# Order of weight splits against block sums and gates in the feed-forwards of a two-layer encoder

## Chip, cores and metric
One core of a Trainium2 chip runs the whole program in one launch. The metric is the device time in microseconds of that core. The engines are PE (TensorE, matmuls), DVE (VectorE), ACT (ScalarE), POOL (GpSimd) and SP (SyncE, which here only issues DMAs). Each runs its own queue of instructions in order; they meet through semaphores.

## What is computed
The trunk has two layers over 256 tokens of width 1024, in float32. Each layer is a feed-forward, a mixer (neighbourhood attention and pooling) and a second feed-forward:

```
def swiglu(h, w_gate, w_up, w_down):
    return (jax.nn.silu(h @ w_gate) * (h @ w_up)) @ w_down

for l in range(DEPTH):                                    # DEPTH = 2
    x = x + 0.5 * swiglu(rms_norm(x, ffn1_norm[l]), w_gate1, w_up1, w_down1)
    ...                                                   # mixer
    x = x + 0.5 * swiglu(rms_norm(x, ffn2_norm[l]), w_gate2, w_up2, w_down2)
```

The inner width is 2816. So the program has four feed-forwards, FF1 and FF2 of each layer.

## The kernel before
**Split numbers.** Every float32 operand is split into a high part (rounded to the matmul's float32r form) and a low part (the rest), and a product is the three matmuls high x high, high x low and low x high (`split_products`, L1397, L1398 and L1400). For a unit of weights (128 x 2048 words, 1 MB) SP loads `w_raw`, ACT writes `w_hi` in two halves (`split_hi`, L627, or with the norm's gains L634), and DVE writes `w_lo = w_raw - w_hi` in two halves (`split_lo`, L984, or L995). The semaphores `raw_ready`, `hi_ready` and `lo_ready` of each slot order these. SP reloads a slot's `w_raw` when the low part of the unit in it is done (`wait_raw_free`).

**Chunks.** A feed-forward is cut into 11 chunks of 256 inner columns. An ordinary chunk takes two gate-and-up units, in slots a and b, one for each half of the 1024 inputs; for each of the two token tiles t PE computes 8 k-tiles (`ordinary`), then ACT takes the silu (`silu_of`, L712), DVE multiplies (`gate`, L1045), PE transposes (L1506), ACT and DVE store the high and low parts (`store_gt_hi` L701, `store_gt_lo` L1051), and PE multiplies with the down unit in slot d (`whole_down`).

**Pairs.** Chunks 0 and 1 go first. Then a loop runs two bodies (`ff_body`, `BODIES = 2`) of four chunks: an ordinary one, a pair whose gate and up products are formed with seven block products instead of eight (`seventh`), and another ordinary one. Chunk 2 is the ordinary one at the start of the first body. The pair needs sums of weight blocks and of activation blocks. Slots e and f serve the pair: e's unit is split, then DVE adds f's raw unit onto e's raw unit (`add_units(e, f)`, L1131), and that sum is split into slot f (`sum_hi`, L643). POOL adds another unit onto f by an accumulating DMA once `sum_ready` says that the first sum is done (L506).

**Activation blocks.** In `ff_stage`, ACT and DVE bring the normed activations to scaled form (`scale_x` L721, `add_low_x` L1085), split them (`x_hi` L731, `x_lo` L1071), sum their blocks in place by four dependent additions on DVE (`sum_blocks`, L1098 to L1107), and split the sums (`s_hi` on ACT, L739, `s_lo` on DVE, L1115). The unsummed blocks serve chunk 2 (PE waits for `x_lo_ready` 4n + 2 ahead of the loop); the summed ones are first read in the pair's products (PE waits for 4n + 4 there).

**Order.** Nothing plans at run time. What runs when on each engine is the order in which the code issues it, written out by hand for ACT, DVE, PE, SP and POOL, with waits at each step. The change touches ACT's and DVE's `ff_body` and `ff_stage`.

Of the kernel before, what the change touches and what calls it, by code (L numbers as in the profile page):

```python
# [103 lines left out]
def trunk(nc, x, ffn1_norm, ffn1_w_gate, ffn1_w_up, ffn1_w_down, mix_norm, w_in, rpb, w_pool,  # L104
# [8 lines left out]
    with ctx:  # L113
# [186 lines left out]
        def raw_no(layer, stage, slot, k):  # L300

            return layer * RAWS_PER_LAYER[slot] + (RAWS_BEFORE[stage][slot] + k)
# [13 lines left out]
        def ord_no(layer, ff, i):  # L316

            return ff_no(layer, ff) * N_ORDINARY + i
# [261 lines left out]
        def _(act):  # L580
# [56 lines left out]
            def sum_hi(slot, raw, ready, used):  # L637

                act.wait_ge(*ready)
                act.wait_ge(*used)  # L640
                for h in range(2):
                    part = slice(h * HALF, (h + 1) * HALF)
                    nc.scalar.activation(w_hi[slot][:, part], w_raw[raw][:, part], ACT.Copy  # L643
                                         ).then_inc(hi_ready[slot], 2)
# [65 lines left out]
            def silu_of(layer, ff, i, t):  # L710
                act.wait_ge(gu_ready[t], ord_no(layer, ff, i) + 1)
                nc.scalar.activation(silu[:, t, :], ps[:, t, 0:FC], ACT.Silu, scale=rstd[:, t, :]  # L712
                                     ).then_inc(silu_ready[t], 1)
# [21 lines left out]
            def s_hi(layer, ff):  # L735

                act.wait_ge(s_summed, 4 * (ff_no(layer, ff) + 1))
                for t in range(TT):
                    nc.scalar.activation(  # L739
                        xs_hi[:, 2 * t + 4:2 * t + 6, :, :].rearrange("p o k q -> p (o k q)"),  # L740
                        normed[:, t, :], ACT.Copy).then_inc(x_hi_ready, 1)
# [11 lines left out]
            def ff_body(layer, ff, j):  # L753
                a, b = ff["g"]
                d, e, f = ff["d"], SLOT_E, SLOT_F
                i = 4 * j + 2
                n = pair_no(layer, ff, j)

                def plain(slot, raw, m, used=None):
                    split_hi(slot, raw, raw_no(layer, ff["stage"], raw, m), used)  # L760

                plain(d, d, 3 * j + 1, (down_used, down_no(layer, ff, i)))
                plain(e, e, 2 * j, (g0_used, ord_no(layer, ff, 2 * j + 1) + 1))
                store_gt_hi(layer, ff, i - 1)
                silu_of(layer, ff, 2 * j + 2, 0)
                sum_hi(f, e, (sum_ready, 3 * n + 1), (gu_ready[1], ord_no(layer, ff, 2 * j + 1) + 1))
                plain(a, a, 2 * j + 3, (g0_used, ord_no(layer, ff, 2 * j + 2) + 1))
                silu_of(layer, ff, 2 * j + 2, 1)
                plain(b, b, 3 * j + 3)
                plain(d, d, 3 * j + 2, (down_used, down_no(layer, ff, i + 1)))  # L770
                copy_m(BANK_X, 7 * n + 1, p1)
                copy_m(BANK_Z, 7 * n + 2, m5)
                sum_hi(e, e, (sum_ready, 3 * n + 2), (m_ready, 7 * n + 1))
                store_gt_hi(layer, ff, i)
                sum_hi(f, f, (t3_loaded, 32 * n + 32), (m_ready, 7 * n + 2))
                act.wait_ge(combined, 7 * n + 1)
                silu_pair(c11, 0, 0)
                sum_hi(a, a, (sum_ready, 3 * n + 3), (m_ready, 7 * n + 3))
                plain(e, b, 3 * j + 4, (m_ready, 7 * n + 5))
                act.wait_ge(combined, 7 * n + 4)  # L780
                silu_pair(p1, 0, 1)
                plain(f, f, 2 * j + 1, (m_ready, 7 * n + 6))
                act.wait_ge(combined, 7 * n + 6)
                silu_pair(m5, 1, 0)
                plain(b, d, 3 * j + 3, (m_ready, 7 * n + 4))
                act.wait_ge(combined, 7 * n + 7)
                silu_pair(u, 1, 1)
                plain(d, e, 2 * j + 1, (down_used, down_no(layer, ff, i + 2)))
                store_gt_hi(layer, ff, i + 1, 1)
                silu_of(layer, ff, 2 * j + 3, 0)  # L790
                store_gt_hi(layer, ff, i + 2)
                plain(a, a, 2 * j + 4, (m_ready, 7 * n + 7))
                silu_of(layer, ff, 2 * j + 3, 1)
                plain(b, b, 3 * j + 5, (down_used, down_no(layer, ff, i + 3)))

            def ff_stage(layer, ff, following=None):
                a, b = ff["g"]
                d = ff["d"]
                stage = ff["stage"]
                scale_x(layer, ff, range(4))  # L800
                for t in range(TT):
                    act.wait_ge(scaled_ready[t], layer * STAGES + (stage + 1))
                silu_of(layer, ff, 0, 0)
                split_hi(a, a, raw_no(layer, stage, a, 1), (g0_used, ord_no(layer, ff, 0) + 1),
                         (stage, layer, 0))
                silu_of(layer, ff, 0, 1)
                split_hi(b, b, raw_no(layer, stage, b, 1), gains_of=(stage, layer, 4))
                scale_x(layer, ff, range(4, KT))
                split_hi(d, d, raw_no(layer, stage, d, 0), (down_used, down_no(layer, ff, 1)))
                x_hi(layer, ff)  # L810
                store_gt_hi(layer, ff, 0)
                silu_of(layer, ff, 1, 0)
                s_hi(layer, ff)
                split_hi(a, a, raw_no(layer, stage, a, 2), (g0_used, ord_no(layer, ff, 1) + 1))
                silu_of(layer, ff, 1, 1)
                split_hi(b, b, raw_no(layer, stage, b, 2))
                with act.Fori(0, BODIES) as j:
                    ff_body(layer, ff, j)
                if ff is FF1:
                    load_params(layer)  # L820
                    load_tables(layer)
                elif layer == DEPTH - 1:
                    load_final_gain()
                split_hi(d, d, raw_no(layer, stage, d, 3 * BODIES + 1),
                         (down_used, down_no(layer, ff, LAST)))
                store_gt_hi(layer, ff, LAST - 1)
                silu_of(layer, ff, 2 * BODIES + 2, 0)
                split_hi(a, a, raw_no(layer, stage, a, 2 * BODIES + 3),
                         (g0_used, ord_no(layer, ff, 2 * BODIES + 2) + 1))
                silu_of(layer, ff, 2 * BODIES + 2, 1)  # L830
                store_last_gt_hi(layer, ff, 0)
                if following:
                    following()
                store_last_gt_hi(layer, ff, 1)
# [136 lines left out]
        def _(dve):  # L971
# [149 lines left out]
            def ff_body(layer, ff, j):  # L1121
# [19 lines left out]
                                                   ALU.mult, ALU.mult).then_inc(pair_gated, 1)  # L1141

                lo(d, 3 * j + 1, d)
                lo(e, 3 * j, e)
                store_gt_lo(layer, ff, i - 1)
                gate(layer, ff, 2 * j + 2, 0)

                dve.wait_ge(raw_ready[f], raw_count(f, raw_no(layer, ff["stage"], f, 2 * j)))
                dve.wait_ge(lo_ready[e], 4 * unit_no(layer, ff["stage"], e, 3 * j) + 5)
# [49 lines left out]
            def ff_stage(layer, ff, following=None):  # L1199
                a, b = ff["g"]  # L1200
                add_low_x(layer, ff, range(4))
                for t in range(TT):
                    dve.wait_ge(scaled_ready[t], layer * STAGES + (ff["stage"] + 1))
                gate(layer, ff, 0, 0)
                unit(layer, ff, a, 1, gains_from=0)
                gate(layer, ff, 0, 1)
                unit(layer, ff, b, 1, gains_from=4)
                add_low_x(layer, ff, range(4, KT))
                unit(layer, ff, ff["d"], 0)
                x_lo(layer, ff)  # L1210
                store_gt_lo(layer, ff, 0)
                sum_blocks(layer, ff)
                gate(layer, ff, 1, 0)
                unit(layer, ff, a, 2)
                gate(layer, ff, 1, 1)
                unit(layer, ff, b, 2)
                s_lo(layer, ff)
                with dve.Fori(0, BODIES) as j:
                    ff_body(layer, ff, j)
                unit(layer, ff, ff["d"], 3 * BODIES + 1)  # L1220
                store_gt_lo(layer, ff, LAST - 1)
                gate(layer, ff, 2 * BODIES + 2, 0)
                unit(layer, ff, a, 3 * BODIES + 3)
                gate(layer, ff, 2 * BODIES + 2, 1)
                store_last_gt_lo(layer, ff, 0)
                if following:
                    following()
                store_last_gt_lo(layer, ff, 1)
# [665 lines left out]
```

## Time and profile before

| | us |
|---|---|
| median of 3 runs (lowest, highest) | 921.59 (921.36, 921.64) |
| profiled execution, its own time | 921.39 |
| its span | 919.6 |
| PE busy (share of span) | 906.5 (99%) |
| PE weight loads busy | 741.1 (81%) |
| DVE busy | 703.5 (77%) |
| ACT busy | 540.1 (59%) |
| HBM read over the span | 179.11 MB, 197 GB/s |

The span is the profiled part between first and last instruction; the execution's own time is 1.8 us longer. Busy time of PE counts matmuls that overlap in its pipeline, so each shows about 0.39 us although they start closer together. The engines wait for each other throughout; idle time matters where it is PE's.

### The profile page before, as it was taken

Reading aid. Unit: us, or ns where it says so; the run is one execution under the profiler, and the core shown is the slowest. Engines: PE = TensorE matmul, PEld = TensorE weight load, DVE = VectorE, ACT = ScalarE, POOL = GpSimd, SP = SyncE. Lnnn points to the kernel's source line nnn. Section 1 sums busy time; section 2 is a strip of 40 time slices with the busy share of each in tenths; the row PEclk is TensorE's granted clock in tenths of the full one; section 3 lists DMA queues with packets and bytes.
Section 4 is the critical chain, followed back from the end, with each engine's and each line's share of the span. In section 5 each row is a group of like instructions: output and inputs, shape, how many; then the busy total and the mean of one; then the engine's idle time right before and its main releaser. Section 6 shows DMA issues by size and latency. Waiting matters only on the chain.

```text
span 919.6 us, 12693 instructions
## 1 busy us (share of the span) xinstructions
PE 906.5 (99%) x4217; PEld 741.1 (81%) x4217; DVE 703.5 (77%) x946; ACT 540.1 (59%) x793; POOL 47.0 (5%) x78
## 2 busy tenths in 40 slices
PE   8999999999999999999999999999999999999997
PEld 6788888887778788888887888888877887888886
DVE  5899688459757898697488987965787588968944
ACT  7765466457638566555385655544675476656633
POOL 1010010010001010100010101010100001001000
PEclk9999999999999999999999999999999999999999
DMA  7876757755245857775268577676434277676631
GB/s 251 302 193 242 274 110 260 240 174 183 92 136 168 290 110 277 237 222 183 91 227 277 127 277 227 207 212 235 138 143 143 82 271 215 217 261 161 246 114 46
DMA packets 131101, 180.76 MB, mean 197 GB/s; under 512 B 7664, under 2 KB 107296, under 8 KB 131056
## 3 DMA queue, kind: packets, MB, share of 16 engines
q1 hardware_dynamic: 117744, 165.43, 52.2%
q0 software_dynamic: 9984, 11.22, 7.4%
q10 hardware_dynamic: 3328, 3.54, 1.2%
q8 instruction: 25, 0.41, 0.2%
q14 instruction: 20, 0.16, 0.1%
HBM read 179.11 MB, written 2.07 MB: 197 GB/s over the span
## 4 chain that ended last, share of the span: by engine, by line
PE 89%; DVE 5%; ACT 3%; DMA 1%; issue 1%; SPq 1%; POOLq 0%; ACTq 0%; POOL 0%; DVEq 0%
PE ps L1397 27%; PE ps L1400 26%; PE ps L1398 26%; PE ps L1506 2%; DVE w_lo L984 1%; PE ps L1458 1%; PE ps L1407 1%; PE ps L1408 1%; DVE xs_lo L1071 1%; PE ps L1480 1%; PE ps L1696 1%; ACT w_hi L634 1%; ACT w_hi L627 1%; PE ps L1712 1%; PE ps L1724 1%
## 5 line engine op out<-in xcount | busy, mean ns | idle before, releaser
L984 DVE TENSOR_TENSOR w_lo<-w_raw,w_hi 128x1024 fp32r<-128x1024 f32 x184 | 216.6, 1218 | 97.2 <-ACT w_hi L627 96.7
L627 ACT ACTIVATE w_hi<-w_raw 128x1024 fp32r<-128x1024 f32 x168 | 167.2, 1049 | 94.3 <-PE ps L1400 94.3
L1397 PE MATMUL ps<-w_hi,gt_hi 128*128 128x512 f32 (+1 forms) x356 | 138.9, 390 | 0.0
L1398 PE MATMUL ps<-w_lo,gt_hi 128*128 128x512 f32 (+1 forms) x356 | 137.7, 387 | 0.0
L1397 PE MATMUL ps<-w_hi,xs_hi 128*128 128x512 f32 x288 | 114.5, 398 | 4.9 <-DVE w_lo L984 4.9
L1400 PE MATMUL ps<-w_hi,xs_lo 128*128 128x512 f32 x288 | 112.4, 390 | 0.0
L1398 PE MATMUL ps<-w_lo,xs_hi 128*128 128x512 f32 x288 | 112.3, 390 | 0.0
L1397 PE MATMUL ps<-w_hi,xt_hi 128*128 128x512 f32 x272 | 110.0, 404 | 0.2 <-DVE xt_lo L1009 0.2
L1400 PE MATMUL ps<-w_hi,gt_lo 128*128 128x512 f32 (+1 forms) x356 | 109.9, 387 | 0.0
L1398 PE MATMUL ps<-w_lo,xt_hi 128*128 128x512 f32 x272 | 106.1, 390 | 0.0
L1400 PE MATMUL ps<-w_hi,xt_lo 128*128 128x512 f32 x272 | 101.1, 391 | 0.0
L995 DVE SCALAR_TENSOR_TENSOR w_lo<-w_raw,gains,w_hi 128x512 fp32r<-128x512 f32 x128 | 88.0, 745 | 15.7 <-ACT w_hi L634 13.3
L634 ACT ACTIVATE w_hi<-w_raw,gains 128x512 fp32r<-128x512 f32 x120 | 76.6, 714 | 4.9 <-PE ps L1400 4.8
L1400 PEld LDWEIGHTS ps<-w_hi,gt_lo 128*128 128x128 f32 x356 | 66.8, 188 | 13.7
L1397 PEld LDWEIGHTS ps<-w_hi,gt_hi 128*128 128x128 f32 x356 | 66.9, 188 | 13.6 <-DVE gt_lo L1051 0.4
L1398 PEld LDWEIGHTS ps<-w_lo,gt_hi 128*128 128x128 f32 x356 | 66.9, 188 | 13.2
L1397 PEld LDWEIGHTS ps<-w_hi,xs_hi 128*128 128x128 f32 x288 | 54.1, 188 | 17.2 <-DVE w_lo L984 6.6
L1400 PEld LDWEIGHTS ps<-w_hi,xs_lo 128*128 128x128 f32 x288 | 54.1, 188 | 11.6
L1398 PEld LDWEIGHTS ps<-w_lo,xs_hi 128*128 128x128 f32 x288 | 54.2, 188 | 10.6
L1397 PEld LDWEIGHTS ps<-w_hi,xt_hi 128*128 128x128 f32 x272 | 51.1, 188 | 14.1 <-issue 3.0
L1400 PEld LDWEIGHTS ps<-w_hi,xt_lo 128*128 128x128 f32 x272 | 51.0, 188 | 11.0
L1398 PEld LDWEIGHTS ps<-w_lo,xt_hi 128*128 128x128 f32 x272 | 51.2, 188 | 8.9
(151 smaller groups left out, 1488.7 us busy)
## 6 DMA issues: line engine op xcount, KB each, us to landing
w_raw<-in_ffn_w_down_dram SPq DMA_DIRECT2D x72, 512.0 KB, 5.4
w_raw<-in_ffn_w_gate_dram SPq DMA_DIRECT2D x62, 512.0 KB, 4.2
w_raw<-in_ffn_w_up_dram SPq DMA_DIRECT2D x62, 512.0 KB, 5.3
w_raw<-in_w_in_dram SPq DMA_DIRECT2D x32, 512.0 KB, 4.7
w_raw_f<-in_ffn_w_gate_dram SPq DMA_DIRECT2D x16, 512.0 KB, 5.3
w_raw_f<-in_ffn_w_up_dram SPq DMA_DIRECT2D x16, 512.0 KB, 6.2
w_raw_e<-in_ffn_w_down_dram SPq DMA_DIRECT2D x16, 512.0 KB, 7.0
w_raw<-in_w_out_dram SPq DMA_DIRECT2D x16, 512.0 KB, 5.1
```

The costliest lines, as they stand in the source:

```text
L627: nc.scalar.activation(w_hi[slot][:, part], w_raw[raw][:, part], ACT.Copy).then_inc(hi_ready[slot], 2)
L634: nc.scalar.activation(w_hi[slot][:, part], w_raw[raw][:, part], ACT.Copy, scale=g).then_inc(hi_ready[slot], 1)
L984: nc.vector.tensor_tensor(w_lo[slot][:, part], w_raw[raw][:, part], w_hi[slot][:, part].bitcast(F32), ALU.subtract).then_inc(lo_ready[slot ...
L995: nc.vector.scalar_tensor_tensor(w_lo[slot][:, part], w_raw[slot][:, part], g, w_hi[slot][:, part].bitcast(F32), ALU.mult, ALU.subtract).t ...
L1071: nc.vector.tensor_tensor(xs_lo[:, 2 * t:2 * t + 2, :, :].rearrange("p o k q -> p (o k q)"), normed[:, t, :], xs_hi[:, 2 * t:2 * t + 2, :, ...
L1397: nc.tensor.matmul(o, hi, wh, start=start, stop=False)
L1398: nc.tensor.matmul(o, hi, wl, start=False, stop=False)
L1400: last = nc.tensor.matmul(o, lo, wh, start=False, stop=bool(stop))
L1407: nc.tensor.matmul(out, hi, w_hi_part, start=start, stop=False)
L1408: nc.tensor.matmul(out, hi, w_lo_part, start=False, stop=False)
L1458: last = nc.tensor.matmul(ps[:, bank, :], xt_lo[:, 0, 4 * a + k, :], w_hi[slot][:, k * BANK:(k + 1) * BANK], start=False, stop=(a, k) == ( ...
L1506: last = nc.tensor.transpose(ps[:, 6, (k * TT + t) * P:(k * TT + t + 1) * P], source[:, t, k * P:(k + 1) * P], ident[:, :])
```

## The change
It moves calls in two functions, on ACT and on DVE alike, and adds and removes none.

In the loop's body, the split of e's first unit goes behind the store of the transposed chunk and the silu (ACT) or gate (DVE) of the body's ordinary chunk, first token tile. Ahead of the loop, both splits of chunk 2's units (`a` and `b`, unit 2), with the silu and gate of chunk 1's two tiles between them, go ahead of `s_hi` on ACT and ahead of `sum_blocks` on DVE.

```diff
@@ ACT, ff_body
                 plain(d, d, 3 * j + 1, (down_used, down_no(layer, ff, i)))
-                plain(e, e, 2 * j, (g0_used, ord_no(layer, ff, 2 * j + 1) + 1))
                 store_gt_hi(layer, ff, i - 1)
                 silu_of(layer, ff, 2 * j + 2, 0)
+                plain(e, e, 2 * j, (g0_used, ord_no(layer, ff, 2 * j + 1) + 1))
                 sum_hi(f, e, (sum_ready, 3 * n + 1), (gu_ready[1], ord_no(layer, ff, 2 * j + 1) + 1))
@@ ACT, ff_stage
                 silu_of(layer, ff, 1, 0)
-                s_hi(layer, ff)
                 split_hi(a, a, raw_no(layer, stage, a, 2), (g0_used, ord_no(layer, ff, 1) + 1))
                 silu_of(layer, ff, 1, 1)
                 split_hi(b, b, raw_no(layer, stage, b, 2))
+                s_hi(layer, ff)
                 with act.Fori(0, BODIES) as j:
@@ DVE, ff_body
                 lo(d, 3 * j + 1, d)
-                lo(e, 3 * j, e)
                 store_gt_lo(layer, ff, i - 1)
                 gate(layer, ff, 2 * j + 2, 0)
+                lo(e, 3 * j, e)
@@ DVE, ff_stage
                 store_gt_lo(layer, ff, 0)
-                sum_blocks(layer, ff)
                 gate(layer, ff, 1, 0)
                 unit(layer, ff, a, 2)
                 gate(layer, ff, 1, 1)
                 unit(layer, ff, b, 2)
+                sum_blocks(layer, ff)
                 s_lo(layer, ff)
```

## Rows read from the trace of the kernel before

**Rows 1.** The page, part 1: busy time, share of the span, instructions.
```profile
PE 906.5 (99%) x4217; PEld 741.1 (81%) x4217; DVE 703.5 (77%) x946; ACT 540.1 (59%) x793; POOL 47.0 (5%) x78
```

**Rows 2.** Waits of PE: total us, times, longest us.
```profile
PE ps L1397 <- DVE w_lo L984: 4.9, 4, 1.4
```

**Rows 3.** Timeline of PE, layer 0, FF1 and FF2: start, length, idle before.
```profile
40.15 0.50 PE L1397 MATMUL ps<-w_hi,xs_hi 128*128 128x512 f32 x1 [1.35 <-DVE w_lo L984]
...
296.91 0.48 PE L1397 MATMUL ps<-w_hi,xt_hi 128*128 128x512 f32 x1
...
306.11 0.62 PE L1400 MATMUL ps<-w_hi,gt_lo 128*128 128x512 f32 x2
...
307.47 0.61 PE L1400 MATMUL ps<-w_hi,gt_lo 128*128 128x512 f32 x2
309.27 0.50 PE L1397 MATMUL ps<-w_hi,xs_hi 128*128 128x512 f32 x1 [1.18 <-DVE w_lo L984]
309.60 0.40 PE L1398 MATMUL ps<-w_lo,xs_hi 128*128 128x512 f32 x1
309.84 0.39 PE L1400 MATMUL ps<-w_hi,xs_lo 128*128 128x512 f32 x1
```

**Rows 4.** Timeline of DVE, layer 0, FF2, ahead of the loop.
```profile
302.03 0.68 DVE L1098 TENSOR_TENSOR normed<-normed 128x512 f32<-128x512 f32 x1
...
307.99 2.36 DVE L984 TENSOR_TENSOR w_lo<-w_raw,w_hi 128x1024 fp32r<-128x1024 f32 x2 [2.70 <-ACT w_hi L627]
310.26 0.48 DVE L1045 SCALAR_TENSOR_TENSOR gated<-ps,rstd_scaled,silu 128x256 f32<-128x256 f32 x1
...
312.93 2.35 DVE L1115 TENSOR_TENSOR xs_lo<-normed,xs_hi 128x1024 fp32r<-128x1024 f32 x2
315.20 2.35 DVE L984 TENSOR_TENSOR w_lo<-w_raw,w_hi 128x1024 fp32r<-128x1024 f32 x2
```

**Rows 5.** Timeline of ACT, layer 0, FF2, ahead of the loop.
```profile
300.00 0.46 ACT L712 ACTIVATE silu<-ps,rstd 128x256 f32<-128x256 f32 x1
304.93 2.01 ACT L739 ACTIVATE xs_hi<-normed 128x1024 fp32r<-128x1024 f32 x2 [4.46 <-DVE normed L1107]
306.84 1.99 ACT L627 ACTIVATE w_hi<-w_raw 128x1024 fp32r<-128x1024 f32 x2
```

**Rows 6.** Timeline of SP's queue: the request for chunk 2's first unit.
```profile
292.60 0.51 SPq L357 DMA_DIRECT2D w_raw<-in_ffn_w_up_dram  x1
```

**Rows 7.** The page, part 6: DMA issues, KB each, us to landing.
```profile
w_raw<-in_ffn_w_up_dram SPq DMA_DIRECT2D x62, 512.0 KB, 5.3
```

**Rows 8.** Busy time in two stretches, layer 0, FF2: first body, second body.
```profile
core 0: us, PE busy (x) PEld busy (x) DVE busy (x) ACT busy (x) POOL busy (x), PEclk, DMA share, GB/s
315.20:353.90 38.70, 38.70 (x175) 31.83 (x173) 37.20 (x38) 22.25 (x28) 2.67 (x2) 1.00 0.71 211
377.90:415.90 38.00, 38.00 (x173) 31.46 (x172) 34.77 (x35) 22.28 (x29) 4.26 (x4) 1.00 0.68 198
```

**Rows 9.** Timeline of DVE and PE, first body, the last unit in f.
```profile
352.74 2.35 DVE L984 TENSOR_TENSOR w_lo_f<-w_raw_f,w_hi_f 128x1024 fp32r<-128x1024 f32 x2
...
353.67 0.39 PE L1400 MATMUL ps<-w_hi_e,xs_lo 128*128 128x512 f32 x1
354.00 0.50 PE L1397 MATMUL ps<-w_hi_f,xs_hi 128*128 128x512 f32 x1
```

**Rows 10.** Timeline of ACT, DVE and PE, second body of the same feed-forward.
```profile
380.74 0.47 ACT L712 ACTIVATE silu<-ps,rstd 128x256 f32<-128x256 f32 x1
...
381.87 2.28 DVE L1131 TENSOR_TENSOR w_raw_e<-w_raw_e,w_raw_f 128x2048 f32<-128x2048 f32 x1
...
398.25 2.36 DVE L984 TENSOR_TENSOR w_lo_e<-w_raw_e,w_hi_e 128x1024 fp32r<-128x1024 f32 x2 [1.08 <-ACT w_hi_e L643]
...
415.05 2.35 DVE L984 TENSOR_TENSOR w_lo_f<-w_raw_f,w_hi_f 128x1024 fp32r<-128x1024 f32 x2
...
418.65 0.39 PE L1397 MATMUL ps<-w_hi_f,xs_hi 128*128 128x512 f32 x1
```

**Rows 11.** POOL's accumulating DMAs (line 506), the line on their landing.
```profile
DMA to landing us min/median/max: 6.1/7.2/10.2
```

## The prediction, made before the changed kernel was run

> **What bounds the kernel now.** I read the page's first section, then what TensorE waited for, then the timelines around those waits. PE is busy 906.5 us of a span of 919.6 [rows 1]. Busy time alone proves little, so the spacing counts: two equal places of a down projection, six matmuls apart, start at 306.11 and 307.47 [rows 3], 1.36 us or 0.227 us a matmul, with nothing between them. So PE's queue is the bound, and only time in which it stands still can be won by a reordering. Its largest wait is for DVE's `w_lo` of an ordinary unit: 4 times, 4.9 us together [rows 2]. There are four feed-forwards, and each has this wait once, at the first matmul of the loop's first body. In the second feed-forward (layer 0, FF2) the last matmuls of the down projection start at 307.47, so the next could start at 307.47 + 2 x 0.227 = 307.92; it starts at 309.27, and the one behind it 0.33 instead of 0.23 later [rows 3]. Each such stall costs 1.35 + 0.10 = 1.45 us, in the first feed-forward 0.17 more, since its idle time is 1.35 and not 1.18 [rows 3]. All four: 4 x 1.45 + 0.17 = 6.0 us.
>
> Why does the low part of chunk 2's first unit come so late? DVE's queue up to 307.99 [rows 4]: four block sums from 302.03, a gate, and then 2.70 us idle until the split's high part is there. ACT's queue [rows 5]: silu at 300.00, done about 300.36; the high part of the summed blocks (`s_hi`) at 304.93, held by the sums; only then the unit's high part at 306.84, and DVE follows 1.15 us later. The unit waits for block sums it does not use.
>
> **Part 1: chunk 2 ahead of the sums** (twice in ff_stage). Nothing is added or dropped; I replay both queues with the spacings that the rows give.
> ACT: behind the silu, a's split starts at 300.36. Its raw data was requested at 292.60 [rows 6] and lands in about 5.3 us [rows 7], so 297.9. Its old contents are free once PE has done k-tile 3 of chunk 1's second half, about 299.9 by the row at 296.91 [rows 3] plus 12 x 0.23 plus one latency. Two halves take 1.91 (the distance 304.93 to 306.84 of two equal operations [rows 5]). The next silu needs PE's end of the chunk, about 302.7, and b's split runs from about 303.2 to 305.2.
> DVE: gate 302.03 to 302.43; a's low part (2.27, from 307.99 to 310.26 [rows 4]) to 304.70; gate (310.26 to 312.93 is a gate and an equal split, so 0.40) to 305.10; b's low part to 307.37. PE wants a at 307.92 and b 2.7 us later: 3.2 us to spare. The stall goes in full.
> Then the sums: 2.90 from their start to the start of s_hi (302.03 [rows 4], 304.93 [rows 5]), so s_hi starts at 310.27; `s_lo` starts 1.15 later at 311.42 and takes 2.27, to 313.69. The loop's first split, d, started on DVE at 315.20 [rows 4] and now starts at 313.69, if ACT has it: s_hi to 312.18, first half of d ready for DVE at 313.33. Behind s_hi on ACT stand d's split and the body's gt_hi and silu; PE wants d only after two products of 5.4 us. So DVE's whole chain moves up 1.51, because its idle 2.70 becomes 1.18. PE waits for the summed blocks only ahead of its first block product, three times 24 x 0.227 = 5.44 and some transposes after 307.92, so at about 324.7; s_lo has 11 us of cover, and without it would cost one for one.
> SP: the loads behind a's and b's low parts (`free(a, 3j+3)`, `free(b, 3j+3)`) go out about 5.7 us earlier, behind e, d and f in the same queue. Their own users come only after e's. What they could cost is bandwidth taken from d, e and f, which were requested first; at the one end that is 0, at the other it eats the 1.5 that DVE's chain gains. I take 0, because a load lands in about 5.3 us [rows 7] and those are out 4 us before. POOL's accumulating DMA waits for the e+f sum and moves with DVE's chain.
>
> **What is late next.** In the first body DVE is nearly the bound itself: 37.20 us busy out of 38.70 [rows 8]. At the pair's last unit f, DVE starts the low part at 352.74 and PE takes it at 354.00, when by the matmul at 353.67 it could have come at 353.90 [rows 9]. There PE is tied to DVE, so what survives this point is DVE's gain, 1.51, not PE's 1.45 (first feed-forward: 1.62). Hence 1.5 us for each feed-forward, 6.0 together. Bounds: DVE gaining only half (0.75 each) gives 3.0; DVE gaining 0.25 more removes this small stall of 0.1 + 0.1 too, 4 x 1.68 = 6.7.
>
> **Part 2: e's split behind gt and gate in every body.** First body: both orders have DVE full, so the e+f sum starts after the same work. ACT: d's high part to 314.1, `gt_hi` to 314.6, silu to 315.0, e's first half at 316.1; DVE: d to 315.96, gt_lo 316.56, gate 316.96, e to 319.23. The sum starts there as it would in the old order; price 0. Had the order stayed, gt_lo would come 2.27 later, but still ahead of PE's 319.3.
> Second body: here it costs DVE something, because e's split used to fill the time in which DVE waited for PE's transposes. Old: silu at 380.74, sum at 381.87 [rows 10]. New: silu done 381.10, e's low part from 382.25 to 384.52, sum at 384.52: 2.65 us later. Behind it stand everything DVE does up to the next wait, ACT's high part of f, POOL's accumulating DMA (landing in 10.2 us at most [rows 11]; ACT takes it 13 us behind), and SP's next load into b. At e's second low part DVE used to wait 1.08 for ACT at 398.25 [rows 10]; that absorbs as much, leaving about 1.5 late. The tightest user is f's last low part: 415.05 becomes 416.6, its first half done at 417.7; PE takes it at 418.65 [rows 10]. 0.9 us is left, and 1.5 at the unit before it. Price 0; uncovered it is one for one. If all 2.65 came through, 1.7 a feed-forward.
>
> **One rule weighed.** The second matmul after the stall follows at 0.33, the third at 0.24 [rows 3]; it does not run faster to catch up. A stall's end is therefore an end for everything behind.
> The Trainium skill, "TensorE: Matmul & The Clock Gate", section "Back-to-back issue gap", gives about 131 ns per matmul of 512 columns as what a real stream sustains. By that, PE would have 0.1 us a matmul in reserve, and the sum would be 0.
>
> **Sum.** Profiled execution 921.39 (span 919.6 and 1.8 around it). 921.39 - 6.0 = 915.4. It lies 0.2 below the median 921.59, so the new median is 915.4 to 915.6; I take **915.6**. Less than 0.2% (1.8 us) either way is what a measurement here cannot tell from no change.
>
> **Rivals.**
> 1. DVE or ACT gains less than PE, and the difference returns as a wait in the first body at f. For: the tie at 354.00. Against: the idle that disappears is plain. At 0.75 each: 918.4.
> 2. Second body, slower: e's split ahead of the sum delays the pair chain, PE waits at f's last low part. It decides from 0.9 us of lateness, and eats the whole gain from 0.9 + 1.5 = 2.4 us; the chain starts with 2.65. For: DVE is busy 34.77 of 38.00 there [rows 8]. Against: the 1.08 wait. If nothing is absorbed, 4 x 1.7 = 6.8 against 6.0: 922.2, slower; together with rival 1's loss 925.2.
> 3. Another condition holds the first body at 309.27 (raw data, an accumulation bank), so nothing is won: 921.4. Against: the row names DVE, and by the half of its 2.27 from 307.99 DVE's first half ended at 309.13, just before PE's start.
> 4. PE has reserve and had caught up anyway, so no change: 921.4. The spacing speaks against. (By the Trainium skill's 131 ns above, this one would hold; the trace does not agree.)
>
> **Chances.** Forecast 0.82; rival 1: 0.08; rival 2: 0.05; rival 3: 0.04; rival 4: 0.01. Faster by over 0.2%: forecast and rival 1, 0.90. Same: 0.07 (3, 4 and half of 2). Slower: 0.03 (the rest of 2). Range 914.7 to 918.2: below it the small stall of 6.7, above it most of rival 1.
>
> **What would show it.** The four waits of PE for `w_lo` of 1.2 to 1.35 us gone; DVE idle between sums and s_lo about 1.2 instead of 2.7; the same small wait for f in first bodies, about 0.2; e+f sums of the second bodies about 2.6 us after the gate, yet no PE wait there. Wrong if PE waits over 0.3 us in a second body, or if the loop still starts over 0.3 us after the first down projection.

## The result, and the profile after

The changed kernel takes 916.02 us in the median of 6 runs (915.74 to 916.33), the kernel before 921.50 beside it (921.35 to 921.72): a ratio of 0.9939, 95% interval 0.9929 to 0.9950, or 5.5 us less. The forecast was 915.6.

The waits of PE's matmuls in the changed kernel, in the form of [rows 2] (total us, times, longest us). The row with 4 times and 4.9 us is gone. The list shows no wait in the loop now; a wait of PE as short as the one at f has no row of its own and is read from the starts below:

```profile
PE ps L1833 <- DVE zeros L972: 1.5, 1, 1.5
PE ps L1397 <- DVE xt_lo L1009: 0.8, 1, 0.8
PE ps L1540 <- DVE xt_lo L1009: 0.6, 2, 0.4
```

These three are in the start and at norms, not in the changed code. In the chain that ended last PE's share is 94% here, after 89%. In the trace before, the chain runs through DVE and ACT ahead of each of the four loops. Here it does so ahead of none, and leaves PE only later in the first feed-forward, at f (84.02). The share itself proves little, though: a second profile of the same changed kernel (run a2 below) gives 88%. There the chain of the last feed-forward leaves PE at f and goes back through DVE and ACT to the block sums. The page's line of the changed kernel, that of a2, and two pieces of a2's chain:

```profile
PE 94%; DMA 2%; DVE 2%; ACT 1%; SPq 1%; issue 1%; POOLq 0%; DVEq 0%; POOL 0%; ACTq 0%
```
```profile
PE 88%; DVE 4%; ACT 3%; issue 2%; DMA 2%; SPq 1%; DVEq 0%; POOLq 0%; ACTq 0%; POOL 0%
...
755.43 0.61 DVE normed L1098
...
799.43 1.14 DVE w_lo_f L984
```

PE's timeline at the same place as [rows 3] (layer 0, FF2; start, length, no idle time):

```profile
306.67 0.62 PE L1400 MATMUL ps<-w_hi,gt_lo 128*128 128x512 f32 x2
307.12 0.39 PE L1397 MATMUL ps<-w_hi,xs_hi 128*128 128x512 f32 x1
307.35 0.39 PE L1398 MATMUL ps<-w_lo,xs_hi 128*128 128x512 f32 x1
```

The first matmul of the loop follows the down projection at 0.45 us, two spacings, and the next one at 0.23, so the slow restart is gone with the wait. DVE's timeline there, to be laid beside [rows 4]:

```profile
301.24 0.47 DVE L1045 SCALAR_TENSOR_TENSOR gated<-ps,rstd_scaled,silu 128x256 f32<-128x256 f32 x1
301.63 2.35 DVE L984 TENSOR_TENSOR w_lo<-w_raw,w_hi 128x1024 fp32r<-128x1024 f32 x2
...
306.56 0.68 DVE L1098 TENSOR_TENSOR normed<-normed 128x512 f32<-128x512 f32 x1
...
310.54 2.36 DVE L1115 TENSOR_TENSOR xs_lo<-normed,xs_hi 128x1024 fp32r<-128x1024 f32 x2 [1.13 <-ACT xs_hi L739]
312.82 2.35 DVE L984 TENSOR_TENSOR w_lo<-w_raw,w_hi 128x1024 fp32r<-128x1024 f32 x2
...
315.69 0.47 DVE L1045 SCALAR_TENSOR_TENSOR gated<-ps,rstd_scaled,silu 128x256 f32<-128x256 f32 x1
316.08 2.35 DVE L984 TENSOR_TENSOR w_lo_e<-w_raw_e,w_hi_e 128x1024 fp32r<-128x1024 f32 x2
318.47 2.29 DVE L1131 TENSOR_TENSOR w_raw_e<-w_raw_e,w_raw_f 128x2048 f32<-128x2048 f32 x1
```

The reader is to see two things. The unit's low part starts before the sums, 5.5 us ahead of PE, and DVE's idle time is 1.13 where it was 2.70. And the sum at 318.47 starts 2.39 us behind the start of e's low part, while anything else that follows such a split starts 2.27 behind it: 0.12 us more.

To compare stretches whatever happened before them, I take the time from the first matmul of the first down projection to the start of the second body in this feed-forward. It was 302.48 to 374.16 before, 71.68 us, and is 301.68 to 371.89 now, 70.21: 1.47 us less. Measured alike, the other three gain 1.41, 1.46 and 1.40, together 5.7. What follows in a feed-forward, from the second body on, takes the same in both kernels (75.99 us before, 75.98 now, up to the first down projection behind the second body).

### The profile page after: what moved, and what is told of

Read it like the earlier page. It is cut to its first block, busy times and chain, and to the rows that moved or that the text cites. A ratio compares the mean times of both kernels' runs of the same rounds, so it can differ in the third digit from the quotient of the medians.

```text
span 914.5 us, 12693 instructions
## 1 busy us (share of the span) xinstructions
PE 905.3 (99%) x4217; PEld 741.0 (81%) x4217; DVE 704.0 (77%) x946; ACT 539.3 (59%) x793; POOL 47.1 (5%) x78
## 4 chain that ended last, share of the span: by engine, by line
PE 94%; DMA 2%; DVE 2%; ACT 1%; SPq 1%; issue 1%; POOLq 0%; DVEq 0%; POOL 0%; ACTq 0%
PE ps L1397 28%; PE ps L1400 28%; PE ps L1398 28%; PE ps L1506 2%; DMA w_raw<-in_ffn_w_up_dram 1%; PE ps L1458 1%; PE ps L1407 1%; PE ps L1408 1%; PE ps L1480 1%; PE ps L1696 1%; PE ps L1712 1%; PE ps L1724 1%; PE ps L1740 1%; DMA w_raw_f<-in_ffn_w_up_dram 1%; SPq L376 0%
```

## The experiments

Each kernel is the kernel before or the changed kernel with the edit shown. Runs e1 to e4 ran together (the kernel before at 921.74 beside them), so did the changed kernel again, e1 again, e5 and e7 (921.87), and e6 and e8 (921.65). Code is cut: `...` stands for arguments, and a comment gives the real call where it matters.

**e1: part 1 alone.**
```diff
@@ changed kernel, ff_body, on ACT and DVE: back to the old order
+                plain(e, e, 2 * j, ...)      # lo(e, 3 * j, e) on DVE
                 store_gt_hi(layer, ff, i - 1)
                 silu_of(layer, ff, 2 * j + 2, 0)
-                plain(e, e, 2 * j, ...)
```


> Part 1 alone: chunk 2's splits ahead of the sums on ACT and DVE, e's split left where it was in the loop's bodies. Theory A (part 1 gives everything; part 2 costs a little, because the e+f sum then stands right behind e's low part and waits 0.12 us for its end, on a chain that in the first body is tied to PE): all four start waits gone, the wait at f in the first bodies 0.12 shorter, 4 x 0.12 = 0.5 us faster than the changed kernel, so 915.5; the e+f sums of the second bodies back to where they were. Theory B (part 2 is what keeps DVE's early move from being lost, for instance through the store of the low gated part): a wait of PE for gt_lo shows up in the first body, 916.5 to 918.

Measured: 915.58 (ratio 0.9933, 0.9919 to 0.9946). No wait for gt_lo appears in a body. The stretch above takes 301.14 to 371.22, 70.08 us. DVE's rows at the sum of the first body:

```profile
316.82 0.68 DVE L1051 TENSOR_TENSOR gt_lo<-ps,gt_hi 128x512 fp32r<-128x512 f32 x1
317.42 0.47 DVE L1045 SCALAR_TENSOR_TENSOR gated<-ps,rstd_scaled,silu 128x256 f32<-128x256 f32 x1
317.81 2.28 DVE L1131 TENSOR_TENSOR w_raw_e<-w_raw_e,w_raw_f 128x2048 f32<-128x2048 f32 x1
```

Here e's low part, which starts at 314.55 and takes 2.35, has been over for 0.9 us when the sum comes up, and the 0.12 is gone. So all of the gain is part 1's.

**e2: part 2 alone.** The counterpart: ff_body as changed, ff_stage as before.


> Part 2 alone: e's split behind store and gate in each body, the order ahead of the loop as before. Theory A: the four start waits stay (4.9 us), the first bodies' tie at f costs 0.12 more each, so 921.5 + 0.5 = 922.0, no wait of PE in the second bodies. Theory B: some gain of its own, 920 to 921. The rival of the prediction (second bodies run late): over 923.

Measured: 922.11 (ratio 1.0005, 0.9996 to 1.0014), 0.4 above the kernel before beside it. The four waits stay, and the stretch takes 302.82 to 374.61, 71.79, 0.11 more than before:

```profile
PE ps L1397 <- DVE w_lo L984: 4.9, 4, 1.3
```

The interval holds 1, so by the times alone it is no difference; the stretch in the trace has the expected sign and size. Second bodies show no wait: the rival of late second bodies did not come.

**e1 and the changed kernel side by side.**


> The changed kernel once more, to stand beside part 1 alone on the same chip and to show whether the 0.58 us by which its first profile was late before the first loop (33.64 against 33.06 us at the first down projection) belongs to it. Theory: it is the start's own scatter, and this profile shows some other value from 33.0 to 33.7; median 5.5 to 6.0 us under the kernel before. Rival: 33.6 again, as something in the changed program makes the start late.

> Part 1 alone once more, beside the changed kernel. Theory A: 0.4 to 0.6 us under it (the 0.12 us at the e+f sum of each first body). Rival: the same within 0.1, and the earlier difference was scatter between sessions.

Measured: the changed kernel 915.96 (915.93 to 916.25; ratio 0.9937), part 1 alone 915.46 (915.25 to 915.68; 0.9931). The two ranges of five runs do not touch: part 2 costs 0.5 us. By the stretches of the first profiles it is 0.10 to 0.13 in each of the four feed-forwards. The start of the first down projection, the last point ahead of any changed code that matters, in the kernel before, the changed one and the changed one again:

```profile
33.06 0.50 PE L1397 MATMUL ps<-w_hi,gt_hi 128*128 128x512 f32 x1
```
```profile
33.64 0.50 PE L1397 MATMUL ps<-w_hi,gt_hi 128*128 128x512 f32 x1
```
```profile
33.10 0.50 PE L1397 MATMUL ps<-w_hi,gt_hi 128*128 128x512 f32 x1
```

In all twelve profiles of this study it lies between 32.98 and 33.68, by no pattern that follows an edit. So 0.6 us of a single execution is the start's scatter, not the change.

**e3: ACT's half of part 1 alone.**
```diff
@@ kernel before, ACT, ff_stage; nothing else
                 silu_of(layer, ff, 1, 0)
-                s_hi(layer, ff)
                 split_hi(a, a, raw_no(layer, stage, a, 2), (g0_used, ord_no(layer, ff, 1) + 1))
                 silu_of(layer, ff, 1, 1)
                 split_hi(b, b, raw_no(layer, stage, b, 2))
+                s_hi(layer, ff)
```


> Only ACT's half of part 1: s_hi behind chunk 2's splits on ACT; DVE keeps the block sums ahead of them, and the bodies stay as before. If what made chunk 2 late was ACT's wait for the sums (theory A), DVE needs no reorder: it goes from the sums to the gate and the low part of a without the 2.7 us idle, is ready 1.4 us ahead of PE, and finds s_hi ready at s_lo. DVE's chain then gains 2.7 instead of 1.5 us, which also lifts the tie at f in the first bodies (0.15 wait and 0.1 restart each): 4 x (1.45 + 0.22) = 6.7 us off 921.5, 914.8, no small wait for f left. Theory C (the DVE reorder is what gives the gain, as 2.9 us of sums stand ahead of the low part): a start wait of up to 1 us each stays, 917 to 919.

Measured: **914.55** (914.43 to 914.85; ratio 0.9920, 0.9907 to 0.9934), the lowest median of all. DVE, with its order as before, has no idle time from the sums to the loop:

```profile
300.63 0.68 DVE L1098 TENSOR_TENSOR normed<-normed 128x512 f32<-128x512 f32 x1
...
303.80 2.35 DVE L984 TENSOR_TENSOR w_lo<-w_raw,w_hi 128x1024 fp32r<-128x1024 f32 x2
306.07 0.47 DVE L1045 SCALAR_TENSOR_TENSOR gated<-ps,rstd_scaled,silu 128x256 f32<-128x256 f32 x1
306.46 2.34 DVE L984 TENSOR_TENSOR w_lo<-w_raw,w_hi 128x1024 fp32r<-128x1024 f32 x2
308.73 2.35 DVE L1115 TENSOR_TENSOR xs_lo<-normed,xs_hi 128x1024 fp32r<-128x1024 f32 x2
311.00 2.35 DVE L984 TENSOR_TENSOR w_lo<-w_raw,w_hi 128x1024 fp32r<-128x1024 f32 x2
```

The low part starts at 303.80 and PE needs it at 306.52, with its first half (1.22 long) done 1.5 us before. `s_hi`, which ACT starts at 303.56, was finished long ago when DVE comes to `s_lo`. The tie at f is gone as well; PE takes f with the ordinary length of 0.39, 1.3 us after its first low half is done:

```profile
348.54 2.35 DVE L984 TENSOR_TENSOR w_lo_f<-w_raw_f,w_hi_f 128x1024 fp32r<-128x1024 f32 x2
...
351.01 0.39 PE L1397 MATMUL ps<-w_hi_f,xs_hi 128*128 128x512 f32 x1
```

The stretch takes 301.08 to 371.02, 69.94, 1.74 less than before. The other half, the sums behind the splits on DVE with `s_hi` still ahead of them on ACT, was not tried: by the code, each engine would wait for the other and never go on.

**e4: ACT's half with part 2.**


> ACT's half of part 1 together with part 2. Theory A: with DVE 1.2 us further ahead, the tie at f is lifted, so the 0.12 us that part 2 costs on DVE is hidden: the same as ACT's half alone, 914.8. If part 2 costs anything in the second bodies, this is slower than ACT's half alone by that much.

Measured: 914.69 (914.52 to 914.99; 0.9922), 0.14 above e3 and with ranges that overlap; the stretch 69.93. Where DVE is ahead, part 2's cost is hidden.

**e5: 0.57 us more on DVE in the changed kernel.**
```diff
@@ DVE, ff_body
                 gate(layer, ff, 2 * j + 2, 0)
+                nc.vector.tensor_tensor(pad[:, :], zeros[:, 0:PAGE_PAD].bitcast(F32),
+                                        zeros[:, 0:PAGE_PAD].bitcast(F32), ALU.add)
                 lo(e, 3 * j, e)
```


> The changed kernel with one useless DVE addition (128 x 480, about 0.57 us of DVE's time) ahead of e's low part in each body. Theory A (tie at f in first bodies, 0.87 us of slack in second ones): 0.57 comes through in each of four first bodies and nowhere else: 4 x 0.57 = 2.3 us slower than the changed kernel, 918.3. Rival (no tie, DVE has room in both): no change, 916. Rival (second bodies tied too): 4.6 us slower.

Measured: 918.28 (917.96 to 918.70), 2.3 over the changed kernel beside it. The stretch of the first body grows by 0.60 (301.64 to 372.45, 70.81), in the four feed-forwards together by 2.3, and nothing is lost in second bodies. So the size is what the theory said, but not the place. PE is already 0.39 late at 330.06, behind the transposes of the ordinary chunk; in the first feed-forward the trace puts the same wait down to ACT's copy of a block product (L746). I had not named that meeting point. Only the rest is lost at f:

```profile
330.06 0.49 PE L1399 MATMUL ps<-w_hi,xs_hi 128*128 128x512 f32 x1
...
352.31 0.50 PE L1399 MATMUL ps<-w_hi_f,xs_hi 128*128 128x512 f32 x1 [0.17 <-DVE w_lo_f L984]
```

**e6, e7, e8: the same addition once, twice and three times a body, in the kernel without the tie (e4).**
```diff
@@ DVE, ff_body; e6 the first, e7 the first two, e8 all three
+                nc.vector.tensor_tensor(pad[:, :], ...)     # ahead of lo(e, 3 * j, e)
+                nc.vector.tensor_tensor(pad[:, :], ...)     # ahead of add_units(e, b)
+                nc.vector.tensor_tensor(pad[:, :], ...)     # ahead of add_units(a, e)
```


> ACT's half of part 1 with part 2, with one useless DVE addition (0.57 us) ahead of e's low part in each body. Theory A (0.86 us of slack at f in all bodies): hidden, 914.7 as without it. Rival (chain tied to PE elsewhere): 2.3 us or 4.6 us slower.

> ACT's half of part 1 with part 2 (no tie in first bodies), with two such useless additions in each body: one ahead of e's low part, one ahead of the e+b sum, 1.14 us together. Its profile without them shows 0.86 us between the end of f's first low half and PE's use of it, in first and second bodies alike. Theory A: 1.14 - 0.86 = 0.28 us and about 0.1 for the restart come through in all eight bodies: 8 x 0.38 = 3.0 us over the 914.7 without them, 917.7. Rival (the second bodies absorb it by other waits): 1.5 us over, 916.2. Rival (slack is larger than read): no change.

> The same kernel with three such additions in each body, the third ahead of the a+e sum, 1.71 us together. Theory A: 1.71 - 0.86 = 0.85 and 0.1 for the restart in all eight bodies, 7.6 us over 914.7: 922.3, which is slower than the kernel before. This prices the prediction's second rival: how late the pair's chain must be to eat the gain. Rival (second bodies absorb): 3.8 over, 918.5.

Measured: 914.90 (914.69 to 914.96), 916.45 (916.40 to 916.57) and 920.77 (920.38 to 921.70), so 0.2, 1.8 and 6.1 us over e4's 914.69. (e4 is of another group; the kernel before stood at 921.65 to 921.87 in all of them.) One is hidden; two and three come out lower than expected. The size was misread, not the place. PE's rows at f in e7, then in e8, first and second body:

```profile
351.18 0.39 PE L1404 MATMUL ps<-w_hi_e,xs_lo 128*128 128x512 f32 x1
351.48 0.50 PE L1401 MATMUL ps<-w_hi_f,xs_hi 128*128 128x512 f32 x1
...
415.88 0.39 PE L1404 MATMUL ps<-w_hi_e,xs_lo 128*128 128x512 f32 x1
416.15 0.50 PE L1401 MATMUL ps<-w_hi_f,xs_hi 128*128 128x512 f32 x1
```
```profile
352.13 0.39 PE L1406 MATMUL ps<-w_hi_e,xs_lo 128*128 128x512 f32 x1
352.92 0.50 PE L1403 MATMUL ps<-w_hi_f,xs_hi 128*128 128x512 f32 x1 [0.40 <-DVE w_lo_f L984]
...
418.15 0.50 PE L1403 MATMUL ps<-w_hi_f,xs_hi 128*128 128x512 f32 x1 [0.39 <-DVE w_lo_f L984]
```

In e7 f starts 0.30 and 0.27 behind the matmul ahead of it instead of 0.23, and with the slow restart each body loses about 0.2; eight bodies make 1.6, against 1.8 measured. Two sizes were misread. The first stands in e4's own DVE row:

```profile
314.73 2.36 DVE L984 TENSOR_TENSOR w_lo_e<-w_raw_e,w_hi_e 128x1024 fp32r<-128x1024 f32 x2 [0.27 <-ACT w_hi_e L627]
```

With e's split behind the silu on ACT, DVE has to wait for its high part, and the first addition fell partly into that. In e4 e's low part starts 0.74 behind the start of the gate ahead of it, in e7 0.96, so the addition's 0.57 moved it by 0.22 only, and both additions move f's low part by 0.79. The second is the slack. Wherever PE is held at f in these traces, it starts 1.26 to 1.28 behind the start of f's low part. In e4 it starts 1.99 behind, so the slack is 0.72 and not the 0.86 of the expectation:

```profile
349.13 2.35 DVE L984 TENSOR_TENSOR w_lo_f<-w_raw_f,w_hi_f 128x1024 fp32r<-128x1024 f32 x2
...
351.12 0.39 PE L1397 MATMUL ps<-w_hi_f,xs_hi 128*128 128x512 f32 x1
```

So 0.79 - 0.72 = 0.07 is left, and e7's first body shows it: 0.30 - 0.23. The third addition adds nearly its full 0.57. In e8 f starts 0.79 behind the matmul ahead of it, 0.56 late, and the restart costs 0.1 more; by the stretches first bodies lose 0.75 to 0.97 and second ones 0.72 to 0.77, together 6.2. First and second bodies lose nearly alike, so the rival in which second bodies absorb more falls.

## Why the prediction was right, step by step

**The start waits.** All four gone, each with its restart. That the unit waited for sums it does not use was the cause, and e3 sharpens it: what held the unit was ACT's wait in front of it, not the 2.9 us of sums on DVE. PE gained 1.45 at this point in layer 0's FF2 and 1.66 in the first feed-forward (forecast 1.62).

**DVE's chain moves up 1.51.** Against the start of the down projection (302.48 before, 301.68 now) the loop's first split moved from 315.20 to 312.82, by 2.38 - 0.80 = 1.58. The idle 1.18 came out as 1.13.

**The tie at f.** Right, and it set the size. f's low part moved from 352.74 to 350.48, 2.26 - 0.80 = 1.46, and PE's use of it from 354.00 to 351.75, 2.25 - 0.80 = 1.45. DVE lost 0.12 on the way, between 312.82 and 350.48. That is the term that the prediction had at 0. In this feed-forward PE's gain at the start and DVE's at f are the same to 0.01, so it can't tell which of them counts. The first one can: its 1.66 shrink to 1.45 at f, DVE's gain there, and PE's wait at f grows. In the trace before and in the changed kernel's, f starts 0.31 and 0.52 behind the matmul ahead of it:

```profile
84.58 0.39 PE L1400 MATMUL ps<-w_hi_e,xs_lo 128*128 128x512 f32 x1
84.89 0.50 PE L1397 MATMUL ps<-w_hi_f,xs_hi 128*128 128x512 f32 x1
```
```profile
83.50 0.39 PE L1400 MATMUL ps<-w_hi_e,xs_lo 128*128 128x512 f32 x1
84.02 0.50 PE L1397 MATMUL ps<-w_hi_f,xs_hi 128*128 128x512 f32 x1
```

With the tie lifted (e3) the four stretches gain 7.05 together; the bound of the prediction for that case was 6.7. e5 adds that PE and DVE's chain also meet earlier in the body, a place that the prediction did not have.

**Part 2 in the first body, "price 0".** Wrong by 0.12 us a feed-forward, 0.5 in all (e1 against the changed kernel). The order of work on DVE is full either way, as I said, but I counted durations and not the wait in between: the sum overwrites e's raw unit and waits for the semaphore of the low part that read it. With a store and a gate between the two, that part is long over. Directly behind it the sum starts 0.04 us after its end (316.08 + 2.35 = 318.43, and 318.47), where an unrelated operation starts 0.08 before the end of the one ahead. The same spacing stood in the trace before, in the four block sums that wait for each other: 0.72 apart for a length of 0.68 to 0.69, where an unrelated operation starts 0.60 after one. That it is this wait was read from the code and the spacings; no run took the wait alone away.

**Part 2 in the second body.** Counted from the body's start (374.16 before, 371.89 now) the e+f sum moved from 7.71 to 10.48, 2.77 later where 2.65 was forecast (the same 0.12); e's second low part 24.09 to 25.70 and f's last 40.89 to 42.49, 1.6 later where 1.5 was forecast; no wait on PE. Where the prediction gives the sums as 2.6 us behind the gate, its own replay makes 3.0, and 3.17 were measured (379.20 and 382.37). The slack at f was there but smaller than the forecast 0.9: f's low part starts at 414.38 and PE takes it at 416.37, 1.99 behind, where a held PE comes 1.27 behind, so 0.72 was left. e5 took only 0.18 of it, as DVE's wait for ACT hid the rest of its addition there as well; e7 and e8 find the edge.

**Loads and POOL, "0".** The earlier loads cost nothing that shows; no wait for a DMA entered PE's list in the loop, and between d's low part and f's DVE lost no more than the 0.12.

**The rule on spacing.** The 131 ns of the Trainium skill's "TensorE: Matmul & The Clock Gate" ("Back-to-back issue gap") would have meant that the change gives nothing. The traces do not agree: the matmuls of the changed kernel follow each other at 0.23 us too, and removing the four stalls (1.45, and 1.66 in the first feed-forward) gave back 5.5 to 5.9 us. So PE has no such reserve here.

**The sum.** 4 x 1.5 = 6.0 forecast; 5.5 measured in the first comparison, 5.9 in the second (921.87 against 915.96), 5.7 by the stretches. The changed kernel stood still (916.02 and 915.96); the kernel before moved, with medians of 921.50 to 921.87 in four groups, so a difference of 0.4 between two such comparisons says nothing. The mis-sized term was part 2, at 0 instead of 0.12 each. It was nearly made up by another small error, since DVE's chain came 1.58 forward and not 1.51; that the sum is so close is in part luck.

## To carry to other kernels

When an engine's queue has a wait that its next items don't need, look first at which single queue holds them; moving one item on that queue can be worth more than moving the producer too (e3 against e1: 914.55 and 915.58), because DVE then sums while ACT splits, and finds `s_hi` ready (in the changed kernel DVE still stands 1.13 us between the sums and `s_lo`, in e3 not at all). In a tight stretch, find the next place where the freed engine meets its supplier, since that tie decides what of the gain stays. And an operation placed directly behind the one whose signal it needs loses the overlap with its end (0.12 us here), so leave an unrelated one between them.

## What the hardware showed that was not expected

After even a wait of 0.02 us at f the first matmul shows 0.50 instead of 0.39 us and the next one follows at 0.33 instead of 0.23 us (e1: 351.09 and 351.42): the 0.1 us of a restart was the same after 1.2 us. It is not the wait alone that brings it: behind the small transposes in the changed kernel, with no wait named, the first matmul shows 0.48 and the next follows at 0.31 (354.96 and 355.27).
